# A hybrid decoder layer on eight cores: held loads, selection matmuls, VectorE denominators, DMA transposes

## What is computed

```
h    = rmsnorm(x, g1)
q,k,v,u = h @ w_in                       # 512 columns each; q, k with rotary
y_a  = MoBA(q, k, v)                     # 8 heads x 64, key blocks of 256: own block (causal)
                                         # plus the 3 best past blocks by q . mean(k of block)
y_p  = (trailing means over 2/4/8/16 of u, minus u) @ w_pool + b, times a scale
x1   = x + rmsnorm([y_a, y_p] @ w_out, g2)
a    = causal_conv3(rmsnorm(x1, g3) @ w_up) + b      # 2 x 2816 columns
out  = x1 + rmsnorm((silu(a_gate) * a_val) @ w_down, g4)
```

## Time and profile before

| | |
|---|---|
| three runs | 905.28, 906.23, 906.93 us; median 906.23 us |
| the profiled execution | 908.53 us, span 907.0 us on its slowest core (core 0) |
| busy, share of the span | PE 90%, DVE 56%, ACT 45%, POOL 32% |
| granted PE clock, mean of core 0 | 0.970 of full speed |
| HBM | 104.99 MB read, 16.84 MB written |

### The profile page before, as it was taken

One profiled execution on the slowest core, in us unless ns is written; L12 is line 12 of the kernel. 1 busy time (PEld: TensorE's weight loads), 2 busy tenths in 40 slices (PEclk: granted clock), 3 DMA queues, 4 the chain that ended last, 5 costly groups with the idle time before them and its releaser, 6 DMA issues.

```text
span 907.0 us, 13527 instructions; the slowest of 8 cores (898.1 to 907.0 us)
## 1 busy us (share of the span) xinstructions
PE 818.4 (90%) x4084; PEld 374.8 (41%) x4084; DVE 510.0 (56%) x654; ACT 411.4 (45%) x655; POOL 292.8 (32%) x358
## 2 busy tenths in 40 slices
PE   1877897978996999998799999999999999999994
PEld 1334344434442444443344444444444444444442
DVE  4515736644632255578758877733257778783322
ACT  3036168427773877865545444411024444542100
POOL 5412412331331133334535554430014344432000
PEclk9987999899997999999989999999999999999998
DMA  8972221422162423437546866942224453431221
GB/s 213 198 211 60 70 60 40 102 51 71 35 95 55 106 84 128 139 111 192 116 106 112 130 107 110 210 93 99 94 70 70 73 89 71 70 116 44 97 93 46
DMA packets 42998, 91.58 MB, mean 101 GB/s; under 512 B 14704, under 2 KB 19312, under 8 KB 42672
## 3 DMA queue, kind: packets, MB, share of 16 engines
q0 software_dynamic: 18992, 59.88, 31.8%
q1 hardware_dynamic: 23936, 30.84, 11.2%
HBM read 104.99 MB, written 16.84 MB: 134 GB/s over the span
## 4 chain that ended last, share of the span: by engine, by line
PE 75%; DVE 6%; issue 5%; DMA 4%; ACT 4%; POOL 3%; SPq 2%; POOLq 0%; DVEq 0%; ACTq 0%
PE ps L716 31%; PE ps L770 17%; PE ps L611 7%; PE ps L592 5%; PE ps L542 5%; PE ps L464 4%; PE ps L670 3%; DMA MEM<-MEM 3%; SPq L103 2%; ACT MEM L608 1%; DVE MEM L687 1%; DMA MEM<-x 1%; PE ps L451 1%; POOL MEM L408 1%; PE ps L598 1%
## 5 line engine op out<-in xcount | busy, mean ns | idle before, releaser
L716 PE MATMUL ps<-MEM 128*128 128x512 bf16 x1408 | 307.9, 380 | 0.4 <-ACT MEM L748 0.3
L716 PEld LDWEIGHTS ps<-MEM 128*128 128x128 bf16 x1408 | 137.6, 98 | 167.1 <-issue 4.0
L608 ACT ACTIVATE MEM<-ps 128x512 bf16<-128x512 f32 (+1 forms) x320 | 161.0, 534 | 88.2 <-PE ps L592 36.0
L723 ACT ACTIVATE MEM<-ps,MEM 128x1024 f32<-128x1024 f32 x88 | 105.9, 1204 | 142.6 <-PE ps L716 139.3
L770 PE MATMUL ps<-MEM 128*128 128x512 bf16 x704 | 152.3, 379 | 0.0
L750 POOL TENSOR_TENSOR MEM<-MEM 128x1024 bf16<-128x1024 f32 x44 | 104.4, 2372 | 134.2 <-DVE MEM L736 76.8
L726 DVE SCALAR_TENSOR_TENSOR MEM<-ps,MEM 128x1023 f32<-128x1023 f32 x88 | 112.8, 1282 | 46.3 <-ACT MEM L723 45.6
L611 PE MATMUL ps<-MEM 128*128 128x512 bf16 (+1 forms) x320 | 112.9, 356 | 10.8 <-ACT MEM L608 9.1
L592 PE MATMUL ps<-MEM 72*128 72x512 bf16 (+1 forms) x320 | 113.0, 361 | 6.2 <-DMA MEM<-MEM 5.9
L729 DVE SCALAR_TENSOR_TENSOR MEM<-ps,MEM 128x1022 f32<-128x1022 f32 x88 | 112.7, 1281 | 8.6
L770 PEld LDWEIGHTS ps<-MEM 128*128 128x128 bf16 x704 | 68.8, 98 | 83.1 <-issue 0.3
(11 more groups left out here) (81 smaller groups left out, 700.5 us busy)
## 6 DMA issues: line engine op xcount, KB each, us to landing
MEM<-w_up_r POOLq DMA_DIRECT2D x44, 512.0 KB, 6.2
MEM<-x POOLq DMA_DIRECT2D x28, 512.0 KB, 5.3
x1s<-MEM POOLq DMA_DIRECT2D x16, 512.0 KB, 3.5
MEM<-x1s SPq DMA_DIRECT2D x16, 512.0 KB, 3.4
out<-MEM SPq DMA_DIRECT2D x16, 512.0 KB, 2.6
MEM<-w_down POOLq DMA_DIRECT2D x22, 256.0 KB, 4.5
MEM<-MEM SPq DMA_DIRECT2D x135, 32.0 KB, 2.1
MEM<-rden SPq DMA_DIRECT2D x30, 128.0 KB, 3.3
```

The lines of the kernel that those rows point to most:

```text
L608: op("act", lambda e, c0=c0, b=b, p=p: e.activation(out=PT[p][:, c0:512], in_=bk[b][:, c0:512], func=AF.Exp, scale=SCALE), rd=[bank[b]], w ...
L716: op("pe", lambda e, c=c, half=half, pr=pr, ws=ws, tb=tb: e.matmul(bk[2 * pr + tb], lhsT=wu[ws][:, c, half * 128:(half + 1) * 128], rhs=HY ...
L723: op("act", lambda e, pr=pr, ch=ch, ts=ts: e.activation(out=tA[ts], in_=PS[pr][:, :], func=AF.Identity, scale=cwb[:, ch, 2:3], bias=cwb[:, ...
```

## The change

- Loads: the first weight loads wait for x tile 1 instead of tile 2; w_qk 1 and 3 and the seven block-indicator copies wait for the last norm of group 0; x and rotary tables of later groups wait for the first matmul that reads the group before; in `sec1` each x tile waits for the output projection of the tile before.
- Group 0's q/k rows are moved by 32 selection matmuls (identity columns) and 16 ACT copies instead of 32 DMAs. The units run k0, q0, k1, q1. Group 1's norms get the best priority of all (`P_NORM`).
- Denominators: two 32x32-block transposes on DVE around a 64x16 reciprocal, and one product, per head. The copies, the DMAs, the HBM tensor, POOL's product and the last pair's special case go.
- Band matmuls of 143 columns that overlap the next tile take the place of pairs of 128 columns: 76 instead of 124.
- Tiles 8 to 15 in `prep` and all 16 tiles in `sec1` are transposed by a DMA on SP instead of PE.
- `vu1` copies values with one ACT operation instead of two. In `sec1` the second Square goes to DVE for tiles 0 to 11 and the residual add goes to POOL for tiles 12 to 15, which use one PSUM pair (2) while the first up units take pairs 0, 1, 3 in turn.

```diff
+P_NORM ... = -1000000
-        after_x = list(xsrc[2][1].w)
+        after_x = list(xsrc[1][1].w)
...
@@ prep_norm
-            transposes(tt, xb, hT_b[tt], evac, ring.get())
+            if tt >= 8:
+                transposes_dma(tt, xb, hT_b[tt])
+            else:
+                transposes(tt, xb, hT_b[tt], evac, ring.get())
         def transposes_dma(tt, xb, dst_b):
             sc.dma_t("sp", "tr%d" % (tt % 2), HY[:, :, tt * 128:(tt + 1) * 128], xn[tt % 2], rd=[xb], wr=[dst_b])
@@ qk_unit
+            if G == 0:
+                for pr in range(2):
+                    b = ring.get()
+                    for j in range(4):
+                        h, s = 2 * pr + j // 2, j % 2
+                        op("pe", lambda e, b=b, j=j, h=h, s=s: e.matmul(
+                            bk[b][32 * j:32 * j + 32, :], lhsT=ident[:, 32 * h:32 * h + 32], rhs=stg[k_][s],
...
+                    for j in range(2):
+                        op("act", lambda e, b=b, j=j, pr=pr: e.copy(out=dst[0:64, 4 * hg + 2 * pr + j, :],
...
@@ attn, end of a head
-                    dma("sp", "dn%d" % k2, [(den4[:, i2, 4 * r:4 * r + 4], dnr)], rd=[buf("dnr%d" % k2)], nbytes=4000,
...
-                    op("dve", lambda e, i2=i2: e.reciprocal(out=den4[:, i2, :], in_=den4[:, i2, :]), wr=[dnb], n=64)
...
+                    op("dve", lambda e, pb=pb, d0=d0: e.transpose(out=dT[d0:d0 + 64, :], in_=bk[pb][d0:d0 + 64, :]),
...
+                    op("dve", lambda e, v0=v0, d0=d0: e.reciprocal(
+                        out=rc[v0:v0 + 64, :], in_=dT[d0:d0 + 64, :].rearrange("p (a b) -> p a b", b=32)[:, :, 0]),
...
+                    op("dve", lambda e, v0=v0: e.transpose(
+                        out=dY[v0:v0 + 64, :].rearrange("p (a b) -> p a b", b=32),
+                        in_=rc[v0:v0 + 64, :].unsqueeze(2).to_broadcast([64, 16, 32])), rd=[rcb], wr=[yb])
+                    op("dve", lambda e, h=h, pb=pb, v0=v0: e.tensor_tensor(
                         out=HY[v0:v0 + 64, h // 2, G * 512:(G + 1) * 512], in0=bk[pb][v0:v0 + 64, :],
+                        in1=dY[v0:v0 + 64, :], op=ALU.mult), rd=[bank[pb], yb], wp=[yT_b[G]])
@@ sec1
-            G, s, p = tt // 4, tt % 4, 2 + tt % 2
-            load_x(tt)
+            G, s, p = tt // 4, tt % 4, (2 + tt % 2 if tt < 12 else 2)
+            load_x(tt, mm1[-1:])
...
-            op("dve", lambda e: e.tensor_tensor(out=xs[s], in0=n1a[tt % 2], in1=xs[s], op=ALU.add),
+            op("pool" if tt >= 12 else "dve", lambda e: e.tensor_tensor(out=xs[s], in0=n1a[tt % 2], in1=xs[s], op=ALU.add),
...
+            if tt < 12:
+                op("dve", lambda e: e.scalar_tensor_tensor(
+                    out=xn[tt % 2], in0=xs[s], scalar=1.0, in1=xs[s], op0=ALU.mult, op1=ALU.mult,
+                    accum_out=sq[2][:, tt:tt + 1]), rd=[xsb], wr=[xb, buf("sq2_%d" % tt)], cost=1.45)
...
-            transposes(tt, xb, hT2_b[tt], "act" if tt >= 12 else "dve", 2 * p)
+            transposes_dma(tt, xb, hT2_b[tt])
@@ prep
+            if G == 1:
+                sc.base = P_NORM
...
+                gate = hT_b[4 * G].r[0]
...
-                    load_x(tt)
-                load_rope(G + 1)
+                    load_x(tt, [gate])
+                load_rope(G + 1, [gate])
@@ first up units
-            return u % 2 if u < 10 else (u - 10) % 4
+            return PSEQ[u] if u < len(PSEQ) else (u - len(PSEQ)) % 4
```

More of the change, by code:

```diff
@@ L400, in build, with power @@
         dma("pool", "frp0", [(rpt[0], rope_d[0])], wr=[buf("rp0")], deps=after_x)
[L401 to L407, removed]
+        load_wqk(2, after_x)
+        def power(i, tt):
+            v, y = rv[i][:, tt:tt + 1], rs[i][:, tt:tt + 1]
             op("pool", lambda e: e.tensor_tensor(out=y, in0=v, in1=mhalf, op=ALU.pow),
@@ L410, in rsqrt @@
             return buf("rs%d_%d" % (i, tt))
+        def rsqrt(i, tt):
+            v, s = rv[i][:, tt:tt + 1], sq[i][:, tt:tt + 1]
+            op("pool", lambda e: e.tensor_scalar(out=v, in0=s, scalar1=1.0 / D, scalar2=EPS, op0=ALU.mult, op1=ALU.add),
+               rd=[buf("sq%d_%d" % (i, tt))], wr=[buf("rv%d_%d" % (i, tt))], n=1)
+            return power(i, tt)
         hT_b = [buf("hT%d" % t) for t in range(NT)]
@@ L545, in vu1 @@
             if s == 0:
[L546 to L550, removed]
+                op("act", lambda e: e.copy(
+                    out=VA2[:, tt, :, 0:3:2, :], in_=bk[b].rearrange("p (r two n) -> p r two n", two=2, n=64)),
+                   rd=[bank[b]], wr=[VA_b[tt]], n=512)
             else:
@@ L599, in qk, with pv @@
                        rd=[buf("cst")], wp=[bank[b]], n=128)
+            def pv(n):
+                h, kt = its[n]
+                c0 = max(0, kt - 4 * G) * 128
+                p, pb = n % 4, 2 + h % 2
+                op("pe", lambda e: e.matmul(
+                    bk[pb][:, c0:512], lhsT=VA[:, kt, h // 2, 64 * (h % 2):64 * (h % 2) + 128], rhs=PT[p][:, c0:512],
+                    start=(n % nkt == 0), stop=(n % nkt == nkt - 1)),
+                   rd=[buf("PT%d" % p), VA_b[kt], buf("VAones%d" % (kt // 8))], n=512 - c0, **W(n % nkt == 0, bank[pb]))
             qk(0)
@@ L858, in build @@
         wu_alias[1] = union(["ur%d" % i for i in range(5)])
-        pt_al = union(["PT%d" % i for i in range(4)] + ["rinv0", "rinv1"])
+        pt_al = union(["PT%d" % i for i in range(4)] + ["dT0", "dT1", "dY0", "dY1"])
         wu_alias[2] = wu_alias[3] = pt_al
@@ L864, in build @@
         sc.base = P_FFN
-        for n in range(4):
+        for n in WFIRST:
             load_wu(n)
```

159 lines of the change are left out of this document (73 added, 86 removed).

## The result

The changed kernel takes 845.07 us against 906.41 for the kernel before on the same chip: ratio 0.9322, interval 0.9266 to 0.9379. Slow runs, in which a die's cores run at a lower clock (here one of four, 983.86 us, at 0.81 to 0.83), are left out of every median and ratio. A second measurement, further down, gave 844.63 us and 0.9275 (0.9231 to 0.9319). The profiled execution took 848.77 us, against 908.53 before: 59.8 us less. The forecast was 856 us, in a range from 828 to 890.

A forecast was written before the change was run, and what follows sets the result against it. PE, busy 90% of the span, was the bound, with losses in the mixing part. Gains 16.6, 12.4, 11, 8 and 12.7 less costs 6 and 4 gave -50.7 us from 908.5, so 857.8, predicted 856 against the 906.2 median; range 828 to 890.

The forecast's parts named there:

- 10 us of new costs: Added time on the path: 6 us for DVE's denominator work and 4 us for DMA transpose latency.
- Denominators: Stretch from 262 us: without a DMA between head and product, gain 11 us of 13.4; DVE's added work costs 6.
- The price of a block transpose: DVE, 64x512 float32: taken as 0.69 us, like a copy of that shape; the other end was 3.36 us.
- the 6 us for DVE's added work: Attention: DVE gains 17 us of work spread over 400 us, 6 us of it on the path, bounds 0 and 31.
- rival 2: Attention on groups 0 and 1: VectorE becomes the bound, added work costs 31 us instead of 6; 881 us, chance 0.12.
- DMA transposes: Prep and `sec1`: 24 transposes move from PE to SP, landing in 4.5 us each, costing 4 us on the path.
- The 12.4: Groups 2 and 3, from 142 and 197 us: PE no longer stands at transposes, gain 12.4 us, bounds 0 and 16.4.
- 8 at the end: End of the mixing part, from 402 us: less DVE work and no PE transposes gain 8 us, bounds 2 and 12.
- Start: Up to 122 us: 26 of 49.5 us lost stay; 23.5 gained less 6.9 of PE work, net 16.6 us.
- Group 0's rows: Start: selection matmuls replace SP's row copies, adding 6.9 us to PE; attention begins around 40 us instead of 61.4.
- Rival 3: `sec1` and attention(3): late DMA transposes hold xn buffers and projections, deciding from about 20 us landing; 938 us, chance 0.06.
- the 6.9 us that I charged: Start: 32 selection matmuls of 512 columns at 0.216 us each add 6.9 us to PE.

The follow-up runs named there:

- run 5: The kernel before with only the DVE denominators added: 888.18 us, ratio 0.9791.
- run 3: The changed kernel with denominators through copies, DMAs and HBM again, all the rest kept: 873.6 us, ratio 0.9596 to the kernel before.
- run 6: The kernel before with only the 24 DMA transposes added: 908.9 us, ratio 1.0016.
- run 2: The changed kernel with all transposes on PE again, the rest kept: 879.0 us, ratio 0.9656 to the kernel before.
- run 10: The kernel before with the DVE denominators and the DMA transposes, nothing else: 882.33 us, ratio 0.9728.
- run 1: The changed kernel measured again with no edit: 844.63 us, ratio 0.9275 to the kernel before.
- run 4: The changed kernel with group 0's rows moved by 32 DMAs on SP again: 839.61 us, ratio 0.9227 to the kernel before.
- run 7: The changed kernel with x tiles and rotary tables of groups 2 and 3 not held back: 852.96 us, ratio 0.9406 to the kernel before.
- run 11: The changed kernel without selection matmuls and with the Squares' unread output in the post-norm's buffer: 844.06 us, ratio 0.9299 to the kernel before.

## Why the prediction was right, and where its steps were not

**Direction and size** held: 60 us against 51. Nothing in the second half moved, and the clock is back at 1.00 wherever the pauses went (but at 80, 160 and 380 us). The reading that the gain lies in PE's pauses and low clock of the mixing part is right: 49.4 of the 59.8 us. Of the 46.9 us priced from 142 us on I had let 15.5 stay and put 10 us of new costs on the path; 22.0 are left, 10.0 of them at the end of this core. But the shares of the parts came out otherwise, and that their errors cancelled in the sum was luck.

**Denominators** (gain 11, cost 6). The price of a block transpose, taken from the nearest copy at 0.69, measured 0.71 and 0.70. But the net of 5 us was mis-sized: alone the part is worth 19 us, and undoing it costs 29. The gain was read from one stretch, where DVE stood; alone the part gives 13.3 us there and 6.7 at the end (run 5), and run 3 shows that the round trip also holds PSUM banks through `rinv`. And the 6 us for DVE's added work did not show where I put it: heads of later groups wait for PE, not for DVE (L642 idles 29.5 us for L620). What of rival 2 is there lies from 80 to 100 us, where DVE is busy 18.97 of 20 us and PE loses 7.8 us.

**DMA transposes** (gain 12.4 in groups 2 and 3, part of 8 at the end, 10.4 of PE work, cost 4). The 12.4 rest on a misreading: I took the 20.3 us for which L451 waits for L441 as the cause of the pauses at 142 and 197 us, and only 1.8 us of it lie there. Taken off PE alone, the transposes closed the first pause all the same, opened one ahead of it and hardly touched the second (run 6). The median landing was 3.3 us instead of 4.5; what landings cost on the path ranges from no pause at 380 us on core 6 to 6.4 us and the low clock behind it on the slowest core, around the 4 that I charged. Here the Trainium skill, "VectorE: DVE Perf Modes", section "The three transpose paths", gave 10.5 us for a tile by estimate; the trace does not agree. By that section's prices TensorE is the cheaper place; here, where PE is the bound and each tile also needs a copy out of PSUM, it is 34.4 us dearer (run 2).

That the price of the part depends on the rest was not in the forecast at all: 0 alone, 6 with the denominators, 34.4 with all. The reckoning used above, over the whole span and as a mean of the cores, shows what differs. Pauses are PE's idle time plus (1 - clock) times the span; work is the rest of the span.

| version | span, us | pauses, us | work, us |
|---|---|---|---|
| before | 901.3 | 111.4 | 789.9 |
| run 6, transposes alone | 905.1 | 131.3 | 773.8 |
| run 5, denominators alone | 885.2 | 92.7 | 792.6 |
| run 10, both | 877.3 | 101.2 | 776.1 |
| run 2, all but the transposes (cores 0, 1, 4, 5) | 874.8 | 78.2 | 796.6 |
| run 1, all (the same cores) | 836.3 | 55.1 | 781.3 |

In each pair the DMA transposes take 15 to 17 us of work off PE, more than the 10.4 that I priced. What they do to the pauses changes sign: 20 us more alone, 9 more beside the denominators, 23 fewer with all the rest, most of these at the end (run 2). A sum of terms, each read from the kernel before, has no place for this.

**Start** (gain 23.5 - 6.9). I let 26 us stay, 16.7 of them in the head; 28.5 were lost to 140 us, 17.9 of them in the head. The net was about right, but not by the step that I named first. "Group 0's rows" was that step: I took from the chain that attention waits for SP's row copies, and so credited the selection matmuls. Run 4 shows that they cost more than they give: once the loads are held back and the units of group 1 are ready, PE has work until the copies land. Of the gain, the held loads of groups 2 and 3 are worth 8 to 12 us (run 7); that the rest is due to other work in PE's list is argued from PE's busy time, not tested. The first score matmul at 55.3 instead of 40 us shows the same: it was late, and PE was busy until then.

**Rival 3** decided nothing, but its chain is real: the longest landing of the slowest core, 15.2 us, is as long as the longest in the earlier trace rows and cost 6.4 us of PE, once. I had it decide from landings of about 20 us for every tile; the median stayed at 3.3.

**A small slip.** 60 of the 128-column band matmuls go, not 52; less the added columns that is 2.9 us by the forecast's own price, not 2.3.

**What stays open.** From the two parts together (882 us) to all (845) are 37 us, 41 by the ratios. Undoing the held loads takes back 8 to 12 of these, undoing the selection gives 5, the norms' order nothing. The overlapped band matmuls, the value copies in one operation, the order of loads and of k0 and q0, the PSUM pairs of the first up units, and the placing of adds and Squares were not tried alone. Among these is one that the list of the change leaves out: the Squares of group 1 write their unread output to a rotary buffer instead of xn. How much of 34.4 and 29 us the new order of the lists is, no run here separates.

## What to carry to other kernels

A part's worth depends on the other parts: the same transposes took some 16 us of work off PE in three settings and gave 0, 6 and 34.4 us, since they added pauses in two of them. The queue that they share with the denominators' DMAs is one reason that the waits support, but without those DMAs they gave only 6. A wait at the end of a chain is worth its length only as long as PE has nothing else in its list; when another part of the change fills the list, the remedy for that wait turns into plain cost. So undo each part of a large change on the finished version: of five tried here, three carried the gain, one nothing, and one cost 5 us.

## What was not expected of the hardware

A block transpose of 64x512 float32 on DVE costs what a copy of that shape costs, out of PSUM (712 ns) and out of SBUF with a repeated input (704), against 688 for the copy in the earlier trace rows.

Selection matmuls with 32 output columns run side by side. The timeline of PE, filtered to their line, and the view of that line from 37 to 39 us (duration ns min/median/max, first and last start):

```profile
37.60 0.61 PE L493 MATMUL ps<-MEM 128*32 128x512 bf16 x6
```

```profile
L493 PE MATMUL ps<-MEM x6: 379/384/390, 37.6 to 37.8; 128*32 128x512 bf16 x6
```

Six of them start within 0.2 us and are done in 0.61, where six matmuls at 0.216 us would take 1.3. By this view the 32 cost less than the 6.9 us that I charged; in PE's busy time they make 3.7 to 7.5 us (run 4), still more than they gave. The Trainium skill, "TensorEngine Tiling (Array Packing)", section "Tiling Modes", says that different tiles can run matmuls in parallel; this trace agrees.

A 256 KB transpose by DMA has a short median, on the slowest cores 3.0 to 3.8 us in the changed kernel and its versions with VectorE denominators, 4.2 in run 3 and 4.4 to 5.7 on the kernel before, but a long tail: the longest of 24 took 6.3 to 15.2 us there, and 26.6 us on another core of run 11. In a stretch with a DMA share near 1.0, one such landing was on the path of the slowest core.
